# Two norm chains, row turns between modulation steps, a zero fill issued later, and a panel's weight loads held until the eighth modulation tile

## What is computed

```python
mod_x = silu(c) @ w_ada + b_ada            # c: one vector; w_ada: 1024 x 6144
mod_c = silu(c_ctx) @ w_ada + b_ada
sh1, sc1, g1, sh2, sc2, g2 = split(mod_x, 6)
p_x = modulate(rmsnorm(x,   norm_mix_w), sh1,  sc1)  @ w_in    # 512 x 1024 by 1024 x 2080
p_c = modulate(rmsnorm(ctx, norm_mix_w), csh1, csc1) @ w_in    # 256 x 1024
# modulate(h, shift, scale) = h * (1 + scale) + shift
```

## Time and profile before

| | us |
|---|---|
| runs | 2194.8, 2198.26, 2199.06; median 2198.26 |
| profiled execution | 2182.58 |
| span of its trace | 2180.7 |
| TensorE busy | 2087.6 (96%) |
| TensorE's mean granted clock | 0.984 of 2.4 GHz |
| VectorE, ScalarE, GpSimd busy | 974.0, 495.3, 218.2 |
| DMA | 565.90 MB, mean 259 GB/s |

### The profile page before, as it was taken

One profiled execution on the slowest core, in us unless ns is written; L12 is line 12 of the kernel. 1 busy time (PEld: TensorE's weight loads), 2 busy tenths in 40 slices (PEclk: granted clock), 3 DMA queues, 4 the chain that ended last, 5 costly groups with the idle time before them and its releaser, 6 DMA issues.

```text
span 2180.7 us, 36117 instructions
## 1 busy us (share of the span) xinstructions
PE 2087.6 (96%) x14969; PEld 1030.8 (47%) x14969; DVE 974.0 (45%) x1651; ACT 495.3 (23%) x878; POOL 218.2 (10%) x266
## 2 busy tenths in 40 slices
PE   5959899999999999999999999899999999999998
PEld 2824545333333333333333333688484448777643
DVE  2511535742232223223322345754577625597742
ACT  2400312111111011101110110311126102666560
POOL 1000001112211221122112222200000000000000
PEclk9979899999999999999999999999999999999999
DMA  9972325999999999999999999713121032212200
GB/s 376 337 293 91 146 109 229 415 412 424 418 415 420 423 418 420 423 420 423 418 421 417 421 421 418 286 69 109 39 105 50 1 105 78 97 58 97 97 20 39
DMA packets 111832, 565.90 MB, mean 259 GB/s; under 512 B 16933, under 2 KB 29010, under 8 KB 77938
## 3 DMA queue, kind: packets, MB, share of 16 engines
q1 hardware_dynamic: 88950, 512.93, 58.1%
q0 software_dynamic: 19584, 49.84, 6.4%
q10 hardware_dynamic: 3228, 2.17, 0.3%
HBM read 545.21 MB, written 37.62 MB: 267 GB/s over the span
## 4 chain that ended last, share of the span: by engine, by line
PE 79%; DVE 3%; DMA 3%; issue 1%; ACT 1%; ACTq 0%; POOL 0%; SPq 0%; POOLq 0%; DVEq 0%
PE ps L2425 30%; PE ps L461 11%; PE ps L2395 9%; PE ps L3964 5%; PE ps L2403 5%; PE ps L3863 4%; PE ps L449 3%; PE ps L1649 2%; PE ps L3843 2%; DMA ring<-in_w_gu 1%; PE ps L3395 1%; PE ps L3386 1%; DMA ring<-in_odd_w_in 1%; PE ps L3015 1%; PE ps L3059 1%
## 5 line engine op out<-in xcount | busy, mean ns | idle before, releaser
L2425 PE MATMUL ps<-ring,xeT 128*32 128x512 f32 x6144 | 668.1, 593 | 4.8 <-DMA ring<-in_w_gu 4.1
L2425 PEld LDWEIGHTS ps<-ring,xeT 128*32 128x32 f32 x6144 | 196.3, 110 | 447.2 <-issue 440.4
L2395 PE MATMUL ps<-ring,mT 128*32 128x512 f32 x2048 | 266.6, 592 | 0.0
L2164 DVE TENSOR_TENSOR mT<-ps,spread_bias 128x768 f32<-128x768 f32 x32 | 30.6, 957 | 433.8 <-PE ps L2425 433.8
L2102 ACT ACTIVATE mT<-mT 128x768 f32<-128x768 f32 x32 | 27.0, 843 | 851.0 <-DVE mT L2164 851.0
L461 PE MATMUL ps<-hT_late,ring 128*128 128x256 f32 x704 | 157.7, 383 | 0.4 <-issue 0.4
L2403 PE MATMUL ps<-ring,mT 128*32 128x256 f32 x2048 | 157.4, 379 | 0.0
L461 PEld LDWEIGHTS ps<-hT_late,ring 128*128 128x128 f32 x704 | 135.0, 192 | 22.4 <-issue 3.7
L2403 PEld LDWEIGHTS ps<-ring,mT 128*32 128x32 f32 x2048 | 66.6, 110 | 153.2 <-issue 153.2
L3964 PE MATMUL ps<-ring,mT 128*128 128x512 f32 x256 | 110.4, 592 | 0.0
L1924 POOL DMA_INDIRECT xe<-xn_scratch,idx x93 | 96.5, 1037 | 31.4 <-issue 29.7
(11 more groups left out here) (517 smaller groups left out, 2569.0 us busy)
## 6 DMA issues: line engine op xcount, KB each, us to landing
ring<-in_w_gu SPq DMA_DIRECT2D x128, 2048.0 KB, 11.1
ring<-in_w_down SPq DMA_DIRECT2D x128, 1024.0 KB, 11.5
y_scratch<-zeros POOLq DMA_DIRECT2D x1, 20352.0 KB, 103.3
ring<-in_even_w_in SPq DMA_DIRECT2D x18, 1024.0 KB, 9.3
ring<-in_w_ada SPq DMA_DIRECT2D x32, 512.0 KB, 11.7
ring<-in_odd_w_in SPq DMA_DIRECT2D x16, 1024.0 KB, 7.7
ring<-in_w_ada SPq DMA_DIRECT2D x8, 1024.0 KB, 17.6
ring<-in_w_in SPq DMA_DIRECT2D x8, 1024.0 KB, 20.7
```

The lines of the kernel that those rows point to most:

```text
L2395: mm = nc.tensor.matmul(quad(b, 2 * q + n), acted(k, q, src), w[:, kk, n * BANK:(n + 1) * BANK], start=first, stop=last)
L2425: mm = nc.tensor.matmul(quad(q, c), left(q), part_columns(w, c), start=start, stop=stop)
```

## The change

- SyncE loads only the identity matrix of the constants first, then the vectors, then the first eight modulation tiles, then the rest of the constants, now counted on `wgk_loads`. It then waits until the eighth modulation tile has landed, and goes on with the stream (first panel's tiles and so on).
- The norm runs in two chains: first the four tiles of x, from when x has landed, then the two of the context.
- TensorE turns x between the modulation steps: after each of steps 4 to 7 two channel groups, with ScalarE copying them unscaled to hT. After step 8 it turns the context, three of its four PSUM banks before the modulation rows are turned and the fourth after.
- VectorE applies scale and shift to x in eight passes over hT in place (128x512 each); TensorE's rank-32 products wait for these one by one. ScalarE, no longer VectorE, applies them to the context's eight groups on eviction.
- GpSimd issues the zero fill when the first product of the second panel is done, and waits for it in the second block, after two memsets, no longer in the first.

The first hunk, which removes the helper `vector_tiles`, is left out, and so is most context:

```diff
@@ -624,16 +614,18 @@
         scol_zeroed = signal("scol_zeroed")
...
         mod_ready = signal("mod_ready")
+        h_ready = xn_ready
         j_vec = [psum.job(0, "dve")]
+        j_tr = [psum.job((2, 3, 0)[k % 3], "act") for k in range(KD)]
         j_rows = psum.job(4, "dve")
+        j_trc = [psum.job(b, "act") for b in (5, 6, 7)]
         j_mod = [psum.job(1, "dve")]
+        j_trc.append(psum.job(2, "act"))
         mod_rows = ptok[:, 2, :]
...
         rows_loads = signal("rows_loads")
-        j_tr = []
-        for k in range(KD):
-            j_tr.append((psum.job(2 + k % 3, "act"), psum.job(5 + k % 3, "dve")))
+        context_loads = rows_zeroed
         j_r = psum.job(0, "dve")
@@ -731,9 +723,12 @@
         with nc.Block() as block:
...
             def _(sp):
-                vec_loads.on(sp.dma_start(cst[:], A["cst"]), 16)
+                vec_loads.on(sp.dma_start(ident, A["cst"][:, C_ID:C_ID + P]), 16)
                 sp.wait_ge(zeroed.sem, 2)
                 load_vectors(sp, 1)
+                stream.load(sp, 1, MIX_SLOTS)
+                wgk_loads.on(sp.dma_start(cst[:, C_ID + P:], A["cst"][:, C_ID + P:]), 16)
+                arrived(sp, MIX_SLOTS - 1)
                 stream.load(sp, end_inputs - 4, MIX_SLOTS)
@@ -743,15 +738,14 @@
                 zeroed.on(nc.gpsimd.memset(wgk[:], 0.0))
...
                 rows_loads.on(pool.dma_start(res[:], A["x"][0].rearrange("(t p) n -> p t n", p=P)), 16)
-                rows_loads.on(pool.dma_start(xc[:], A["ctx"][0].rearrange("(t p) n -> p t n", p=P)), 16)
+                context_loads.on(pool.dma_start(xc[:], A["ctx"][0].rearrange("(t p) n -> p t n", p=P)), 16)
...
                 scol_zeroed.wait(pool)
-                pool.wait_ge(mod_ready.sem, 3)
+                p_vp.p1.filled(pool)
                 rows_zeroed.on(pool.dma_start(
...
                     zeros[0:CAP, :].unsqueeze(1).to_broadcast([CAP, (E + XB) * D // BANK, BANK])), 16)
-                rows_zeroed.wait(pool)
@@ -766,20 +760,27 @@
                 act.wait_ge(scol_zeroed.sem, 1)
...
                 scol_ready.on(nc.scalar.activation(scol[:, :, 1], vcol("c_ctx", 0, KD), ACT.Silu))
-                act.wait_ge(rows_loads.sem, 32)
-                for t in range(NT + NTC):
-                    if t:
-                        rms_sum.wait(act)
-                    rms_sum.on(nc.scalar.activation(junk[:], xtile(t), ACT.Square,
-                                                    accum_out=stat[:, t:t + 1]))
-                act.wait_ge(rms_mean.sem, 1)
-                rms_root.on(nc.scalar.activation(stat[:, 16:22], stat[:, 8:14], ACT.Sqrt))
-                act.wait_ge(mod_ready.sem, 3)
-                for k in range(KD):
-                    j = j_tr[k][0]
+                act.wait_ge(rows_loads.sem, 16)
+                for first, end in ((0, NT), (NT, NT + NTC)):
+                    if first:
+                        act.wait_ge(context_loads.sem, 16)
+                    for t in range(first, end):
+                        if t:
+                            rms_sum.wait(act)
+                        rms_sum.on(nc.scalar.activation(junk[:], xtile(t), ACT.Square,
+                                                        accum_out=stat[:, t:t + 1]))
+                    act.wait_ge(rms_mean.sem, 2 if first else 1)
+                    rms_root.on(nc.scalar.activation(stat[:, 16 + first:16 + end], stat[:, 8 + first:8 + end], ACT.Sqrt))
+                for k, j in enumerate(j_tr):
+                    act_out(act, j, hT[:, k, 0:T], bank(j.bank))
+                act.wait_ge(mod_ready.sem, 2)
+                for i, j in enumerate(j_trc):
                     j.filled(act)
-                    j.empty(nc.scalar.activation(hT[:, k, 0:T], bank(j.bank), ACT.Identity,
-                                                 bias=mod1[:, k, 0:1], scale=amix[:, k, 0:1]))
+                    for half in range(2):
+                        k = 2 * i + half
+                        ins = nc.scalar.activation(hT[:, k, T:], ps[:, j.bank, half * TC:(half + 1) * TC], ACT.Identity,
+                                                   bias=mod1[:, k, 1:2], scale=amix[:, k, 1:2])
+                    j.empty(ins)
@@ -812,14 +813,15 @@
             def _(dve):
...
                 j_vec[0].empty(nc.vector.tensor_copy(vec[:], bank(0, 3 * P)))
-                dve.wait_ge(rms_sum.sem, NT + NTC)
-                rms_mean.on(nc.vector.tensor_scalar(stat[:, 8:14], stat[:, 0:6], 1.0 / D, EPS, ALU.mult, ALU.add))
-                dve.wait_ge(rms_root.sem, 1)
-                dve_step.on(nc.vector.reciprocal(stat[:, 24:30], stat[:, 16:22]))
-                dve_step.wait(dve)
-                for t in range(NT + NTC):
-                    xn_ready.on(nc.vector.tensor_scalar(xtile(t), xtile(t), stat[:, 24 + t:25 + t], None,
-                                                        ALU.mult))
+                for first, end in ((0, NT), (NT, NT + NTC)):
+                    dve.wait_ge(rms_sum.sem, end)
+                    rms_mean.on(nc.vector.tensor_scalar(stat[:, 8 + first:8 + end], stat[:, first:end], 1.0 / D, EPS, ALU.mult,
+                                                        ALU.add))
+                    dve.wait_ge(rms_root.sem, 2 if first else 1)
+                    dve_step.on(nc.vector.reciprocal(stat[:, 24 + first:24 + end], stat[:, 16 + first:16 + end]))
+                    dve_step.wait(dve)
+                    for t in range(first, end):
+                        xn_ready.on(nc.vector.tensor_scalar(xtile(t), xtile(t), stat[:, 24 + t:25 + t], None, ALU.mult))
                 j_rows.filled(dve)
@@ -833,14 +835,11 @@
                         out=amix[:, :, v], in0=mod1[:, KD:, v], scalar=1.0, in1=vcol("norm_mix_w", 0, KD),
...
                 mod_ready.wait(dve)
-                mod_ready.on(nc.vector.memset(stat[:, 60:61], 0.0))
-                for k in range(KD):
-                    j = j_tr[k][1]
-                    j.filled(dve)
-                    j.empty(nc.vector.tensor_scalar(hT[:, k, T:], bank(j.bank, TC), amix[:, k, 1:2],
-                                                    mod1[:, k, 1:2], ALU.mult, ALU.add))
-                for j in j_tr[-1]:
+                for k, j in enumerate(j_tr):
                     j.emptied_for(dve)
+                    h_ready.on(nc.vector.tensor_scalar(hT[:, k, 0:T], hT[:, k, 0:T], amix[:, k, 0:1], mod1[:, k, 0:1],
+                                                       ALU.mult, ALU.add))
+                h_ready.wait(dve)
                 w = {b: arrived(dve, blocks(p_qkg, b)) for b in EARLY_ORDER}
@@ -919,22 +918,38 @@
                 j_vec[0].done(mm)
...
-                vector_tiles(pe, j_rows)
+                def turn_x(k):
+                    j = j_tr[k]
+                    j.open(pe)
+                    for t in range(NT):
+                        mm = nc.tensor.transpose(ps[:, j.bank, t * P:(t + 1) * P], xtile(t)[:, k * P:(k + 1) * P], ident)
+                    j.done(mm)
+
+                def turn_context(i):
+                    j = j_trc[i]
+                    j.open(pe)
+                    for q in range(4):
+                        mm = nc.tensor.transpose(ps[:, j.bank, q * P:(q + 1) * P],
+                                                 xtile(NT + q % 2)[:, (2 * i + q // 2) * P:(2 * i + q // 2 + 1) * P], ident)
+                    j.done(mm)
+
+                for k in range(KD):
+                    mm = vector_step(pe, j_rows, k, take(pe)[:, 0, :])
+                    if k < KD - 1:
+                        stream.release(mm)
+                    else:
+                        stream.owe()
+                        j_rows.done(mm)
+                    if 3 <= k < KD - 1:
+                        if k == 3:
+                            pe.wait_ge(xn_ready.sem, NT)
+                        turn_x(2 * k - 6)
+                        turn_x(2 * k - 5)
+                pe.wait_ge(xn_ready.sem, NT + NTC)
+                for i in range(3):
+                    turn_context(i)
                 turn_vector_rows(pe, j_rows, j_mod[0], mod_rows)
-                pe.wait_ge(xn_ready.sem, NT + NTC)
-                for k in range(KD):
-                    jx, jc = j_tr[k]
-                    jx.open(pe)
-                    for t in range(NT):
-                        mm = nc.tensor.transpose(ps[:, jx.bank, t * P:(t + 1) * P], xtile(t)[:, k * P:(k + 1) * P], ident)
-                    jx.done(mm)
-                    jc.open(pe)
-                    for t in range(NTC):
-                        mm = nc.tensor.transpose(ps[:, jc.bank, t * P:(t + 1) * P],
-                                                 xtile(NT + t)[:, k * P:(k + 1) * P], ident)
-                    jc.done(mm)
-                j_tr[-1][0].emptied_for(pe)
-                j_tr[-1][1].emptied_for(pe)
+                turn_context(3)
@@ -944,6 +959,10 @@
                 for j, cols in ((j_r, slice(0, T)), (j_rc, slice(T, W3))):
...
```

(14 more changed lines are left out.)

1 line of the change is left out of this document (removed).

## The result

The changed kernel takes 2220.58 us (median of 4 runs, 2220.25 to 2222.59), the kernel before 2198.66 (2194.8 to 2205.32): ratio 1.0098, 95% interval 1.0073 to 1.0124, so 21.9 us slower. The forecast was 2194.5 with a range of 2176 to 2203. It was wrong in sign and outside its range.

The account below looks back on a forecast made before the run. Tile loads delayed by the zero fill's DMA traffic were taken to hold up TensorE's first 290 us. Gains 6.4 (head) + 20.8 (second group and panel) - 23.4 (fill's new place) = 3.8 us: 2194.5 us, range 2176 to 2203.

Parts of the forecast that it names:

- Part 1: Head, up to the first panel: fewer constants ahead of the modulation tiles and earlier row turns gain 6.4 us (3 to 8).
- SyncE's hold leaves no hole: Head: the remaining constants fill the DMA queue while SyncE waits for the eighth modulation tile; a hole would cut the gain to 3 us.
- Part 2: Second modulation group and second panel: without the fill, the panel starts at C+11.7 (C: group start), not C+32.5; gain 20.8 us.
- Rival 3: Second panel: the 13.25 us wait is not the fill's, so only the head moves; about 2198 us, chance 0.07.
- Part 3: Third modulation group and next stage's start: the moved fill delays tiles and first pooling product; cost 23.4 us, low end 17.7.
- the forecast's even rate: Fill beside the weight queue: remaining 12.1 MB at half of 345 to 407 GB/s, ending at 220 to 230 us.
- Rival 1: Moved fill: drains in about 51 us plus some 10, sparing the pooling product; 2177 us (2172 to 2186), chance 0.25.
- Rival 2: Next stage: broadcast gate rows come last, behind a fill lasting till 240; 4 to 10 us slower, 2202 to 2208, chance 0.13.
- the rival's own sign: Next stage: VectorE waiting for the gate rows g1b or g2b would show that late gate rows set the time.
- the forecast's clock term: Behind the third group's wait: a product runs at a lower clock, 8.88 us against 7.03; cost 1.8 us.

Follow-up runs that it names:

- experiment 1: Changed kernel, with GpSimd not draining its DMAs at the end of the first block: 2198.5 us, ratio 1.0034 to the kernel before.
- experiment 8: Changed kernel with the fill in three pieces and without SyncE's wait for the eighth modulation tile: 2168.65 us, ratio 0.9894 to the kernel before.
- experiment 3: Kernel before with only the whole fill moved to behind the second panel's first product, waited for in the second block: 2217.91 us, ratio 1.012.
- experiment 6: Kernel before with only the fill cut in three pieces, issued at the first panel, second panel and in the second block: 2172.15 us, ratio 0.9906.
- experiment 5: Changed kernel with the fill in three pieces, at the first panel, second panel and in the second block: 2167.27 us, ratio 0.9888 to the kernel before.
- experiment 2: Changed kernel with the same fill issued at the same point from ScalarE's queue, not GpSimd's: 2185.87 us, ratio 0.9974 to the kernel before.
- experiment 4: Changed kernel with the whole fill issued in the second block, behind GpSimd's two memsets: 2202.65 us, ratio 1.0045 to the kernel before.
- experiment 7: Changed kernel with the fill issued early and waited for in the first block, as in the kernel before: 2192.49 us, ratio 1.0004 to it.

## Why the prediction was wrong

**Its failing step is the wait moved to the second block.** The prediction read that edit as "GpSimd waits later" and costed only the fill's traffic. GpSimd waits at the end of the first block all the same, in the drain, and every engine with it. No rival had this. Its price is +21.9 - 7.0 = 14.9 us in the runs, with the uncertainty of the 21.9, and 15.9 in the traces (experiment 1). The 31 us of idle cost only about half their length, because without them the pooling product waits 13.00 us for its matrix. The trace of before could not show the price, but it did show the instruction: on the block's line L731 every engine has a drain, and GpSimd's began at 145.6, just behind the landing of the fill at 145.4. The prediction doesn't use that line. The question it raises, what a drain does with a transfer still outstanding, would have made one more rival: by the forecast's own figures the block's work is done at 183.2 + 19.3 = 202.5 and the fill ends at 220 to 230, so TensorE would stand for 17 to 28 us.

**Part 1, the head: right in its place, a little high.** TensorE's panel was to start at 43.6 to 45.6 and started at 44.11; step 8 ended by 36.04 (34.97 + 1.07), 36.3 forecast; VectorE is next late, at 57.03 (56.4 forecast), with TensorE's gate products waiting 1.90 us for it. The second group started 5.8 us earlier, 6.4 forecast. The eight half-size passes took 3.74 us, not 2.9: 0.47 each, so half the elements did not cost half the time of 0.69. The claim that SyncE's hold leaves no hole holds (experiment 8). At the end of the kernel the head is worth 4.5 to 5.0 by the runs (experiments 3 and 6), 3.7 to 5.9 by the traces at the w_out product. Why the second is less in experiment 6 can be seen in its head: TensorE's row turns are at the 2.4 GHz level from 42.2 us (0.60 us for four), in experiment 3 from 45.4 only, and its second group starts at 112.53 against 114.47, though neither has a fill beside the head.

**Part 2, the second group and panel: right.** Of the wait of 13.25 us, 8.9 were the fill's and 4.4 remain, as forecast. Experiments 3 and 5 show the same 4.40: without the fill panel two starts 13.2 to 13.5 us after its group (121.50 - 108.34; 127.94 - 114.47), forecast 11.7, before 32.5. The gain was 19.3 us, forecast 20.8. Rival 3 is out.

**Part 3, the fill's new place: the mechanism right, its size too low even without the drain.** By experiment 1, whose fill landed at 245.4 and not 220 to 230:

| from the start of the third group | forecast | experiment 1 | changed kernel | experiment 2 |
|---|---|---|---|---|
| end of the third group | 19.3 | 22.2 | 22.7 | 15.7 |
| start of the pooling product | 32.5 | 40.0 | 57.6 | 24.9 |

The forecast carried over 15.2 us for two 1024 KB tiles. In experiment 1 the pool weights and the first pooling matrix came 226.32 - 206.56 = 19.8 us behind the last modulation tile, and that tile itself 3 us later than forecast. The two err the same way, by 7.5 us together. Why each came later, no run separates. The bulk of the fill went as forecast: 7.8 MB by 161 us in the changed kernel (8.7 forecast), and by 220, where the forecast's range for the end begins, all but 0.90 MB there, all but 1.02 MB in experiment 1. What the forecast's even rate left out is the tail: those last 5% took another 19 and 25 us. Rival 1, a fill over after some 51 us, is out: in no run did the whole fill land in less than 99.5 us. Rival 2 said that a fill lasting till 240 makes the kernel 4 to 10 us slower. Experiment 1 is 7.0 slower with a fill till 245, but what TensorE waited for was the pooling matrix. VectorE did wait for the gate rows, 4.43 us, the rival's own sign, and it cost TensorE nothing. So its size came out by luck, all the more as its sum is off: one microsecond for each beyond 227 makes 13 us at 240, not 8, and the kernel would have been 9 to 15 us slower.

**The sum without the drain.** Forecast 3.8 us gained, measured 7.0 lost: a miss of 10.8. Ahead of the third group the gain was 24.1 (210.38 - 186.28) instead of 27.2, which is 3.1: about 0.5 from the head, 1.5 from the group before the panel, and 1.0 from the panel's first product, 9.93 us where 8.88 had been kept. The pooling product was 7.5 later. That is 10.6 at the pooling product. The two drifts behind it nearly cancel: the forecast's clock term of 1.8 us shows as 5.29 against 3.67 us for that product. The drain adds the other 14.9.

One reading is off without bearing on the sum: the first three slices of the page are at 376, 337 and 293 GB/s, not about 400.

## What to carry to other kernels

In this case a wait taken out of a block stayed in it, because GpSimd, which issued the transfer, drains at the block's end: a transfer that is to outlive a block should be issued by an engine whose drain doesn't wait for it (here ScalarE), or be cut so that each piece lands inside its block. Moving a large background transfer only moves the stage that pays for it; cut into pieces that fit the slack between bursts of loads, it left TensorE a wait of 0.16 us in the third group and none for it at the block's end. A fill that must have landed by some point also has to be timed by its last bytes and not by its mean rate. With the same edits to the head the kernel was 22 us slower with the fill whole and late, no different with it whole and early, and 24 us faster with it in three pieces.

## What the runs showed of the hardware

GpSimd's drain lasted 107.9 us behind a transfer of its own that took 107.7 to land, 32.8 behind one of 32.6 (experiment 5) and 0.3 where the program had waited already. ScalarE's drain took 1.05 us with a transfer from its hardware queue outstanding that had 58 us still to go, and SyncE's 0.12 us at 204.1 in experiment 1, with the pooling matrices that it had asked for still to land. By the profile's count the same DMA went in 4.1 KB packets on GpSimd's queue and in 2.0 KB packets on ScalarE's, at nearly equal speed (3.51 and 3.40 MB in 16.5 us), and a pooling matrix asked for beside it landed in 33.7 us in the one case and 18.6 in the other.

The fill of 20.84 MB has a tail in each of these runs: the last 0.8 to 1.1 MB took 17 us (experiment 4), 19 (the changed kernel) and 25 (experiments 1 and 2), with little or nothing in the other queues in the first two.

Unexpected too: VectorE was held while GpSimd issued a large transfer. In experiment 7 the fill's issue (3.23 us from 39.36) falls among VectorE's eight passes over 128x512. They take 6.42 us, 3.74 in the changed kernel, where GpSimd issues nothing beside them. The windows of VectorE on that line, ahead of the issue, within it and behind it (window, length, busy time and instructions, granted clock, DMA share, GB/s):

```profile
38.70:39.36 0.66, 0.66 (x2) 1.00 1.06 410
39.36:42.59 3.23, 3.23 (x2) 1.00 1.05 400
42.59:45.20 2.61, 2.53 (x6) 0.70 1.06 385
```

A pass that lies across an edge counts on both sides. Of the eight, one takes 3.22 us, as long as the issue, and the median is 0.54, as in the changed kernel. The six behind the issue take 2.53 together. The DMA share is 1.05 or more in all three windows, so the traffic itself doesn't tell them apart.

The Trainium skill (SBUF — State Buffer, Who interferes with whom) says that VectorE in some of its modes and GpSimd share a pair of ports, that the one which comes first has it for a whole instruction, and that the other is fully blocked. The trace agrees in kind: one pass of VectorE's lasts as long as the issue (3.22 and 3.23 us) and the others keep their time, so VectorE is stopped, not slowed in proportion. No run shows which mode these passes used.
